# A two-layer pool / mLSTM block in fp32: second FFN pass, when weight slots are awaited, where the gated value is split, and the order of its first tiles

## The reference

```python
def _conv_ffn(h, w_in, conv_w, conv_b, w_out, grid):
    u, g = jnp.split(h @ w_in, 2, axis=-1)            # 1024 -> 2 x 2816
    g = _dwconv_grid(g, conv_w, conv_b, grid)         # 3x3, per channel
    return (jax.nn.silu(g) * u) @ w_out               # 2816 -> 1024

x = x + gt1 * _rms_norm(yx, norm_g[i, 1])
fx = _conv_ffn(_modulate(x, norm_g[i, 2], sh2, sc2), ffn_w_in[i], ...)
x = x + gt2 * _rms_norm(fx, norm_g[i, 3])
```

## Time and profile before

| | us |
|---|---|
| median of 3 runs | 2566.64 (2566.49 to 2570.15) |
| the profiled execution | 2571.05 |
| its span | 2569.1 |
| TensorE busy | 2395.2 (93%) |
| VectorE busy | 1696.2 (66%) |
| GpSimd busy | 902.0 (35%) |
| ScalarE busy | 814.6 (32%) |

### The profile page before, as it was taken

The page is one execution under the profiler, slowest core; times in us unless marked ns, Lnnn a source line. Parts: engine busy times, 40 slices in busy tenths (PEclk is TensorE's granted clock), DMA queues, the critical chain, the costliest instruction groups (busy, mean ns, idle before and its releaser), DMA issues.

```text
span 2569.1 us, 35908 instructions
## 1 busy us (share of the span) xinstructions
PE 2395.2 (93%) x13630; PEld 1948.4 (76%) x13630; DVE 1696.2 (66%) x2160; ACT 814.6 (32%) x1186; POOL 902.0 (35%) x444
## 2 busy tenths in 40 slices
PE   7989999999999999999999998897988889988997
PEld 5557777777777779998899977675777777766774
DVE  4568888888888855543544166246666667788886
ACT  3631111111111145644433333335232322323222
POOL 0012221122122236642211055205555555555453
PEclk9999999999999999999999999998999999999998
DMA  8561222112222246541212387121111011111113
GB/s 347 204 222 41 82 82 82 69 54 82 82 82 82 90 189 230 181 150 56 74 54 69 105 226 202 50 85 47 50 50 41 33 49 49 49 49 49 65 41 131
DMA packets 106688, 255.08 MB, mean 99 GB/s; under 512 B 8928, under 2 KB 62816, under 8 KB 92128
## 3 DMA queue, kind: packets, MB, share of 16 engines
q1 hardware_dynamic: 89024, 228.56, 25.8%
q10 hardware_dynamic: 17568, 25.17, 2.7%
HBM read 223.68 MB, written 30.02 MB: 99 GB/s over the span
## 4 chain that ended last, share of the span: by engine, by line
PE 82%; DVE 6%; ACT 4%; issue 3%; POOL 3%; DMA 2%; SPq 0%; ACTq 0%; DVEq 0%; POOLq 0%
PE ps L733 17%; PE ps L734 16%; PE ps L735 16%; PE ps L1367 5%; PE ps L1369 4%; PE ps L1368 4%; PE ps L1119 2%; PE ps L1121 2%; PE ps L1120 2%; PE ps L1272 1%; PE ps L835 1%; POOL p_s_val L3099 1%; DVE macc_x L2361 1%; PE ps L868 1%; PE ps L770 1%
## 5 line engine op out<-in xcount | busy, mean ns | idle before, releaser
L2998 POOL TENSOR_TENSOR w_lo<-raw,w_hi 128x2048 fp32r<-128x2048 f32 x57 | 266.8, 4681 | 654.2 <-ACT w_hi L1635 293.6
L733 PE MATMUL ps<-hx_hi,w_hi 128*128 128x512 f32 x848 | 338.8, 400 | 2.5 <-ACT mix_out_c L1789 1.0
L735 PE MATMUL ps<-hx_lo,w_hi 128*128 128x512 f32 x848 | 331.5, 391 | 0.0
L734 PE MATMUL ps<-hx_hi,w_lo 128*128 128x512 f32 x848 | 331.3, 391 | 0.0
L2397 DVE TENSOR_TENSOR y_x<-y_x,ps 128x1024 f32<-128x1024 f32 x176 | 214.7, 1221 | 61.7 <-PE ps L735 55.9
L2905 DVE TENSOR_TENSOR y_x<-y_x,ps 128x512 f32<-128x512 f32 x304 | 205.3, 687 | 68.3 <-PE ps L735 68.2
L2379 DVE SCALAR_TENSOR_TENSOR acc<-ps,fcv,acc 128x945 f32<-128x945 f32 (+2 forms) x176 | 215.0, 1222 | 37.1 <-ACT acc L1679 15.9
L2852 DVE SCALAR_TENSOR_TENSOR acc<-ps,fcv,acc 128x945 f32<-128x945 f32 (+2 forms) x176 | 215.1, 1222 | 16.8 <-ACT acc L2092 3.7
L733 PEld LDWEIGHTS ps<-hx_hi,w_hi 128*128 128x128 f32 x848 | 160.0, 189 | 40.3 <-DVE hx_lo L2536 2.5
L735 PEld LDWEIGHTS ps<-hx_lo,w_hi 128*128 128x128 f32 x848 | 159.9, 189 | 34.2
L734 PEld LDWEIGHTS ps<-hx_hi,w_lo 128*128 128x128 f32 x848 | 160.2, 189 | 30.7
(11 more groups left out here) (414 smaller groups left out, 5718.9 us busy)
## 6 DMA issues: line engine op xcount, KB each, us to landing
raw<-in_ffn_w SPq DMA_DIRECT2D x44, 1024.0 KB, 6.6
modw<-in_modw SPq DMA_DIRECT2D x48, 512.0 KB, 7.4
raw<-in_ffn_w SPq DMA_DIRECT2D x44, 512.0 KB, 6.4
f_raw<-in_ffn_w SPq DMA_DIRECT2D x22, 1024.0 KB, 5.1
modw<-in_modw SPq DMA_DIRECT2D x21, 1024.0 KB, 4.8
raw<-in_mlstm_w SPq DMA_DIRECT2D x14, 1024.0 KB, 5.3
fw_raw<-in_ffn_w SPq DMA_DIRECT2D x22, 512.0 KB, 3.7
vch<-v_scr SPq DMA_DIRECT2D x18, 512.0 KB, 4.5
```

The source lines that it names most:

```text
L733: pe.matmul(out, whi, hhi, start=first, stop=False)
L734: pe.matmul(out, wlo, hhi, start=False, stop=False)
L735: return pe.matmul(out, whi, hlo, start=False, stop=last)
L2998: pool.tensor_tensor(w_lo[:, slot, 0:2048], raw[:, slot, 0:2048], w_hi[:, slot, 0:2048].bitcast(F32), ALU.subtract)\
```

## The change

- `free_at` takes the position in the very order that the tile before used: the loop's order, or, when tile 3 is made, the order of tile 2 with its exchanged slots (`fourth`). For the loop that gives 2 for s1, 3 for s2, 4 for s4, 5 for s3, 6 for g2, 7 for u2.
- `gated_low` on GpSimd is gone; VectorE runs `f_low` after `up_second` in every tile, and `last_mod_half` is cut in two parts, one before and one after `gate_first_half`.
- In `first_halves` the q sums stand behind steps 11, 12, 14, 15, 17, 18, 20, 21, and the spread behind step 25.
- g1 and g2 of tile 2 run before `down(0)` (`third_first`). The differences are made in another order and place: all by GpSimd, x21 is shifted and reduced in its own plane, t4 is made before t3, and the weight parts of tile 2 in the order s1, g1, g2, u2, s2, s4, s3.
- SyncE's wait before the first modulation half follows the new counts.

```diff
-MADE_THIRD = ("s1", "u2", "g1", "g2", "s2", "s4", "s3")
+MADE_THIRD = ("s1", "g1", "g2", "u2", "s2", "s4", "s3")
+SUM_STEPS = (11, 12, 14, 15, 17, 18, 20, 21)
...
-def free_at(name):
-    return max(done_at(True, name), done_at(True, THIRD_SLOT[name]), done_at(False, name))
+def free_at(name, fourth=False):
+    if fourth:
+        return done_at(True, {slot: q for q, slot in THIRD_SLOT.items()}[name])
+    return done_at(False, name)
...
-                    if 14 <= step <= 28 and step % 2 == 0:
-                        half_sums("q", 3, (step - 14) // 2)
-                half_spread("q", 3)
+                    if step in SUM_STEPS:
+                        half_sums("q", 3, SUM_STEPS.index(step))
+                    if step == 25:
+                        half_spread("q", 3)
...
+            def third_first():
+                pe.wait_ge(sem("act_moved"), 2 * 4 + SECOND["act_moved"])
+                pe.wait_ge(sem("tap_done"), SECOND["tap_done"] + 8)
+                for name in ("g1", "g2"):
+                    product(name, 2 * 7 + (SECOND["lo_in"] + made_at(True, name)), True)
...
             first_halves()
             second_halves()
+            third_first()
             pe.wait_ge(sem("act_moved"), PLAIN_MOVED + 3)
             down(0, 0, True)
...
                 elif not third:
-                    act.wait_ge(sem("w_in_used"), j * 7 + (SECOND["w_in_used"] + free_at(name) - 7))
+                    fourth = isinstance(j, int) and j == 3
+                    act.wait_ge(sem("w_in_used"), j * 7 + (SECOND["w_in_used"] + free_at(name, fourth) - 7))
...
             half_deviation("q", 3)
-            plain_moved(1, 0)
-            for k in range(KH):
-                act.activation(y_x[:, KH + k, 0:TH], y_x[:, KH + k, 0:TH], ACT.Identity, ...)
+            part_high("s1", 2, True)
             for d in range(KH):
                 high1(d)
+            plain_moved(1, 0)
...
+            for name in ("g1", "g2", "u2"):
+                part_high(name, 2, True)
+            for k in range(KH):
+                act.activation(x21_at[:, k, :], x21_at[:, k, :], ACT.Identity, ...)
...
             pre_half(3, 1, pres["x_pre2b"])
-            for k in (0, 2):
-                dve.tensor_tensor(x_val["t1"][:, k:k + 2, :], ..., ALU.subtract).then_inc(sem("pre_t"), 1)
...
                 f_gate(j - 1, 1 - par)
                 up_second(j, par)
+                f_low(j - 1, 1 - par)
+                if mod_half is not None:
+                    last_mod_part(mod_half, 0)
                 gate_first_half(j)
                 if mod_half is not None:
-                    last_mod_half(mod_half)
+                    last_mod_part(mod_half, 1)
                 f_add(j - 1)
...
-            for k in (0, 2):
-                ... dve.tensor_tensor(x_lo["t3"][:, k:k + 2, :], ..., ALU.subtract).then_inc(sem("pre_lo"), 1)
             f_add(0, True)
...
             up_second(FT - 1, 1, True)
+            f_low(FT - 2, 0)
             f_taps(FT - 1)
...
-            def gated_low(j, par):
-
-                pool.wait_ge(sem("a_hi_ready"), j + (SECOND["a_hi_ready"] + 1))
-                pool.tensor_tensor(fa_lo[:, par, :], fprod[:, par, :], fa_hi[:].bitcast(F32), ALU.subtract)...
-
-            def parts(j, par):
+            def parts(j):
...
                 part_sum("s4", j)
-                gated_low(j - 2, par)
                 part_low("s2", j)
...
             part_low("s1", 2, True)
-            part_low("u2", 2, True)
             out_low(0)
+            for k in (0, 2):
+                pool.wait_ge(sem("pre_t"), pres["x_pre2b"] + 8 + k + 2)
+                moved(x_val["t1"][:, k:k + 2, :], res_h[:, k:k + 2, :], y_x[:, k:k + 2, 0:TH])
...
```

More of the change, by code:

```diff
@@ L1427, in products @@
                     last_mod_columns()
-                product("g1", made("g1"), third)
+                if not third:
+                    product("g1", made("g1"))
                 if last:
                     pe.wait_ge(sem("mod1_done"), FT)
-                if third or last:
-                    product("g2", made("g2"), third)
+                    product("g2", made("g2"))
                 pe.wait_ge(sem("dve_moved"), j * 3 + (summed - 2))
                 if third:
-                    pe.wait_ge(sem("pool_low"), SECOND["pool_low"] + 10)
+                    pe.wait_ge(sem("pool_low"), SECOND["pool_low"] + 12)
                 product("s1", made("s1"), third)
@@ L2355, in last_mod_half @@
                 dve.wait_ge(sem("modw1_in"), 16 * (FT + n))
-                for k in range(KH * h, KH * h + KH):
+                for k in range(KH * h + 2 * e, KH * h + 2 * e + 2):
                     if k == 0:
@@ L2864, in f_low @@
                 dve.wait_ge(sem("a_hi_ready"), j + (SECOND["a_hi_ready"] + 1))
-                if last:
-                    dve.wait_ge(sem("a_lo_ready"), j + SECOND["a_lo_ready"])
                 hi = fa_hi2 if last else fa_hi
@@ L2895, in f_add @@
                     y = y_x[:, d, TH * c:TH * c + TH]
-                    if first and n == 8:
-                        dve.wait_ge(sem("pool_low"), SECOND["pool_low"] + 8)
+                    if first and n in (0, 8):
+                        dve.wait_ge(sem("pool_low"), SECOND["pool_low"] + (10 if n else 8))
                     if n < 2 * KT - 1:
@@ L2934, in _ @@
             up_second(2, 0, True)
+            f_low(1, 1)
             f_add(1)
@@ L3089, in part_sum @@
                 else:
-                    pool.wait_ge(sem("w_in_used"), j * 7 + (SECOND["w_in_used"] + free_at(name) - 7))
+                    fourth = isinstance(j, int) and j == 3
+                    pool.wait_ge(sem("w_in_used"), j * 7 + (SECOND["w_in_used"] + free_at(name, fourth) - 7))
                 s1, s2 = p_val[slot_of(third, "s1")], p_val[slot_of(third, "s2")]
@@ L3162, in _ @@
             for k in (0, 2):
-                pool.wait_ge(sem("pre_hi"), SECOND["pre_hi"] + 7 + k // 2)
-                moved(x_lo["t4"][:, k:k + 2, :], x22_at[:, k:k + 2], x_hi["t4"][:, k:k + 2, :].bitcast(F32))
+                pool.wait_ge(sem("pool_low"), SECOND["pool_low"] + 3 + k // 2)
+                pool.wait_ge(sem("c_shifted"), SECOND["c_shifted"] + 8 + k + 2)
+                moved(x21_at[:, k:k + 2], x21_at[:, k:k + 2], x_val["t2"][:, k:k + 2, :])
+            pool.wait_ge(sem("w_in_used"), PLAIN_DONE + 8)
             for k in (0, 2):
-                pool.wait_ge(sem("pre_hi"), SECOND["pre_hi"] + 1 + k // 2)
+                moved(x_val["t3"][:, k:k + 2, :], x22_at[:, k:k + 2], x12_at[:, k:k + 2])
+            for k in (0, 2):
+                pool.wait_ge(sem("pre_hi"), SECOND["pre_hi"] + 5 + k // 2)
+                moved(x_lo["t4"][:, k:k + 2, :], x21_at[:, k:k + 2], x_hi["t4"][:, k:k + 2, :].bitcast(F32))
+            part_low("u2", 2, True)
+            for k in (0, 2):
                 moved(x_lo["t1"][:, k:k + 2, :], x_val["t1"][:, k:k + 2, :], x_hi["t1"][:, k:k + 2, :].bitcast(F32))
@@ L3174, in _ @@
             part_low("s3", 2, True)
+            for k in (0, 2):
+                pool.wait_ge(sem("pre_hi"), SECOND["pre_hi"] + 7 + k // 2)
+                moved(x_lo["t3"][:, k:k + 2, :], x_val["t3"][:, k:k + 2, :], x_hi["t3"][:, k:k + 2, :].bitcast(F32))
+            parts(3)
             with pool.Fori(0, FT // 2 - 2) as i:
-                parts(i * 2 + 3, 1)
-                parts(i * 2 + 4, 0)
-            parts(FT - 1, 1)
+                parts(i * 2 + 4)
+                parts(i * 2 + 5)
             out_low(FT - 2)
-            gated_low(FT - 2, 0)
             out_low(FT - 1, True)
```

51 lines of the change are left out of this document (16 added, 35 removed).

## The result

| | before | after |
|---|---|---|
| median of the runs | 2566.97 (4 runs, 2566.49 to 2570.15) | 2462.75 (4 runs, 2461.11 to 2463.12) |
| span of the profiled execution | 2569.1 | 2460.4 |

The ratio is 0.959, with an interval of 0.9574 to 0.9607: 104.2 us by the medians, 108.7 between the two profiled spans. The time is shorter than the forecast of 2485 and lies under the range's lower end of 2468. The profiled execution after took 2462.57 us, next to its median; the 4.4 us that I took off the sum for the distance of the execution before to its median had no counterpart.

What follows compares the result with a forecast made beforehand. TensorE, 93% of the span, was taken as the bound, with only idle time and slow clock to win. 60 + 12 + 6 + 3.2 + 1.5 - 1.2 = 81.5 us off 2571.05 gives 2489.5, median 2485; range 2468 to 2512.

Steps and rivals of the forecast that it cites:

- Slots and loop tiles (60): Loop tiles: slots awaited by their own product end the pause before u2; 35.48 to 30.03 a tile, 60 us.
- B: Loop tile keeps a remainder: gate and `f_low` held by GpSimd, 1 to 1.5 us a tile; about 2508, chance 0.2.
- C: Slower: late `f_low` delays the y sums, TensorE pauses in `down` each tile and its clock falls; 2576, chance 0.03.
- D: Loop tiles: silu stays late, as ScalarE's `part_high("s1")` waits for a sum behind the second load; 2560, chance 0.04.
- the forecast's own sign of being wrong (after 20): Loop tiles: the prediction would be wrong if sums of y start after offset 20, counted from a tile's first product.
- Modulation tiles (12): Tiles 14 to 19: VectorE is the bound, 34.7 us a tile against 36.7; gain 12 us.
- Clock behind the modulation pause: Modulation tiles: TensorE waits some 3 us for the first y sum; 8 to 14 slow matmuls cost 1.0 to 2.3.
- Rival A: Modulation tiles without clock fall: about 33 us a tile, 10 us more gain, 2475; chance 0.15.
- Low part on VectorE: `f_low` behind `up_second`: 1.23 us on VectorE, fits loop tiles, not modulation tiles; costs 1.2 in tile 21.
- Start (6): Start of the pass up to u2 of tile 2: earlier q sums and new order give 6 us, bounds 0 and 24.3.
- 3.2 for tile 3: Tile 3: its own pause before u2 falls away, 3.2 us.
- the end (0.3): Last tiles: tile 20 loses slow matmuls, 1.5 us; `f_low(20)` on the chain in tile 21 costs 1.2.

Runs made afterwards that it cites:

- the last kernel: The changed kernel with ScalarE's new order in tile 2 and the gated value's low part back on GpSimd, block still cut: 2451.76 us, ratio 0.9557.

## Why the prediction was right or wrong

The forecast for the profiled execution, 2489.5, is 27 us above the 2462.57 measured. By the terms of its sum:

- **Slots and loop tiles (60): right.** 59.96 measured. The offsets hold too: sum s1 at 7.9 (reckoned 8 to 9.5), silu 11.6 (11.4), gate ended 14.2 (14.5), first y sum 20.0 (19.8); `f_low` started at 15.4 and took 1.23, with 17 to 18 reckoned for its end and 16.6 found. The y sum stands at the forecast's own sign of being wrong (after 20), but it is TensorE's product that sets it. Rivals B, C and D are refuted by the loop's 30.03. The experiments on s1's slot show that the cause is the one named, and that the margin was thin: with the sum 3.4 us later in the tile, u2 waits 0.46 us.
- **Modulation tiles (12): wrong, and this is the failed step.** The prediction put "`modulation 6.7`" into VectorE's cycle, got 33.3, and set 34.7 with the clock's fall. 36.4 was gained: a tile is 30.7. Summing the tile from 2192.21 to 2222.88: y sums 10.51, taps and silu 11.15, gate 2.14, `up_second` and the wait for the high part 1.28, `f_low` 1.14, modulation 2.87, `gate_first_half` 0.60, modulation 0.98. The modulation is 3.85 instead of 6.7; everything else is 26.8, where the forecast had 26.6. The 6.7 came from a trace in which GpSimd, itself late, ran back to back beside the block, and I carried a disturbed duration over into a kernel where the disturbance had moved. With 3.85 the same sum gives 30.5, about TensorE's own 30.03, with no pause to set the clock back: 4 us less in each of six tiles, and the forecast would have been 24 us lower, 2461. GpSimd of the kernel before beside the block of the earlier trace rows, which ran from 2258.16 to 2264.9:

```profile
2258.13 1.29 POOL L3099 TENSOR_TENSOR p_s_val<-f_raw,p_s_val 128x512 f32<-128x512 f32 x1
2259.36 2.44 POOL L3119 TENSOR_TENSOR fa_lo<-fprod,fa_hi 128x1024 fp32r<-128x1024 f32 x1
2261.77 2.88 POOL L3108 TENSOR_TENSOR p_s_lo<-p_s_val,p_s_hi 128x512 fp32r<-128x512 f32 x2
```

- **Clock behind the modulation pause: not reached.** A consequence of the same term: with pauses of 0.2 to 0.6 us the clock stayed at 1.00. The kernel with s1's slot at the fourth position shows that such a fall can happen there: pauses of 2.4 to 2.8 us, three of six with slow matmuls behind. Rival A had the right sign; its 33 rested on the same 6.7.
- **The port.** The gate took 1.27 in a loop tile and 2.22 in a modulation tile, where GpSimd operations start at 2183.18 and 2184.43 (the second took 2.29, where it takes 1.3 alone). The Trainium skill (SBUF — State Buffer, "Who interferes with whom") says a VectorE instruction with two SBUF inputs and a GpSimd one that reads SBUF exclude each other for whole instructions. The trace agrees: 0.48 against 1.3 to 1.5 us for the same `macc_x`. I weighed that rule for `f_low`, where it came to nothing in the loop tiles, and not for the block that it decided.
- **Low part on VectorE: a small loss.** The prediction bounded it as a cost of VectorE time in the modulation tiles and of 1.2 at the end. Both are there: 0.68 a modulation tile, 4.1 us in six, and a `f_low` of 1.22 between `up_second` and the taps of the last tile, where TensorE waits 5.33 instead of 4.20. The medians are 4.4 us apart; the 1.1 of the last tile doesn't show in the profile's end, which is 0.5 shorter.
- **Start (6): right in size, in part by luck.** 5.74 measured from the pass's first product to the y sums of tile 2, and 0.82 more before it, ahead of anything that the change touches in the pass; u2 of tile 2 at 1825.80 for a forecast of 1825. The earlier sums brought 2.2 to 3.3 of it, not the 4.5 reckoned, and g1 and g2 ahead of `down(0)` nothing; what is left belongs to the new order and place of the differences and weight parts, which no run took apart. `keep_a` behind s3's high part held up s2, as the prediction had followed it through ScalarE's queue, without asking what another order there would give: 9 to 11 us.
- **3.2 for tile 3, and the end (0.3).** The 3.2 was counted twice, as tile 3's pause lies in the first of the eleven periods; tile 20's, behind the last mark of the six, was left out. The end measured 5.79: tile 20's pause of 3.15 and its eight slow matmuls, and some slow matmuls fewer behind the last silu, less 1.2 for `f_low`. The two slips leave 2.3 us on the low side; with the 24.4 of the modulation tiles and 0.6 at the start they make up the 27 between forecast and measurement.

## What to carry to other kernels

When an engine's order puts a part that waits ahead of one that others wait for, look at the count on which it waits, product by product; here one slot, awaited three products too long, was worth 100 us. A duration read beside a busy neighbour is not the instruction's own: before it goes into a sum, find the same shape with the neighbour idle, and ask which of the two the changed kernel will have. A short two-input VectorE operation belongs where GpSimd waits for something else.

## What the runs showed of the hardware that was not expected

A 128x256 `SCALAR_TENSOR_TENSOR` with two SBUF inputs took 0.48 us alone and 1.3 to 1.5 beside GpSimd operations of 1.3 that follow one another; its one-input form (`TENSOR_SCALAR`, same shape) took 0.34 alone and 1.38 beside them. Here the price of such a neighbour went by the neighbour's length, and was relatively worst for the shortest operations; the 0.69 of a y sum, with one input in PSUM, stayed between 0.68 and 0.69. And a pause of TensorE does not cost the clock by its length alone. In the traces of this pass no pause up to 1.8 us that found the granted clock at 1.00 was followed by slow matmuls. Two pauses of 2.08 and one of 1.92 were, ones of 1.91 and 2.12 were not; of those of 2.4 to 2.8 some were, of those of 3.1 to 3.3 most, and the one of 3.44 in tile 2 of the last kernel was not. What else decides isn't shown here.
